# Gated DeltaNet layer on one core: the output weights' second half is prepared behind stream tiles q and v0 instead of between them

## The reference, cut to what matters

```
mod = silu(c) @ ada_w + ada_b;  shift, scale, gate = split(mod)
h = rms_norm(x) * (1 + scale) + shift
q, k, v, z, b, a = split(h @ w_in)         # 8 heads; q, k 128 wide, v, z 256 wide
q, k, v = silu(causal_conv4(q | k | v));   q, k = l2_norm(q) / sqrt(128), l2_norm(k)
per head, chunks of the sequence: invert (I + tril(beta k k^T * decay)), then
   S = state;  u = T (beta v - ... k S);  o = q S + (q k^T * decay) u;  S = S * g + k^T u
o = rms_norm(o) * silu(z)
out = rms_norm(x + gate * (o @ w_out))
```

## Time and profile before

| | |
|---|---|
| median of 3 runs | 1201.17 us (1200.78 to 1202.61) |
| the profiled execution | 1203.63 us, its span 1201.8 us |
| TensorE busy | 1114.4 us, 93% of the span |
| VectorE, GpSimd, ScalarE busy | 836.7, 599.9, 448.1 us |
| TensorE's granted clock, mean | 0.972 of full |

### The profile page before, as it was taken

How to read it: one execution, slowest core, us unless ns; L and a number is a source line. 1 busy time by engine, 2 the same in 40 slices (tenths; PEclk the granted TensorE clock), 3 DMA queues, 4 the chain that set the end, 5 groups by cost and what they waited for, 6 DMA issues and landing times.

```text
span 1201.8 us, 19507 instructions
## 1 busy us (share of the span) xinstructions
PE 1114.4 (93%) x5628; PEld 920.6 (77%) x5628; DVE 836.7 (70%) x1888; ACT 448.1 (37%) x1038; POOL 599.9 (50%) x819
## 2 busy tenths in 40 slices
PE   3896899999999999999999999999999999999984
PEld 2665688887888788887888788887888788887863
DVE  4776586776858586775858586685868677685835
ACT  4642333333242433433333333334243333334333
POOL 2353544565444744466345754456444853456413
PEclk9897899999999999999999999999999999999988
DMA  9922222213122321223221221223221222213103
GB/s 311 326 58 60 63 58 62 55 57 81 40 62 57 80 57 44 56 60 76 55 62 40 81 65 43 62 55 81 57 59 43 79 56 55 62 40 97 33 25 123
DMA packets 150754, 88.31 MB, mean 73 GB/s; under 512 B 29446, under 2 KB 145320, under 8 KB 150696
## 3 DMA queue, kind: packets, MB, share of 16 engines
q1 hardware_dynamic: 150696, 87.73, 26.6%
HBM read 78.28 MB, written 9.44 MB: 73 GB/s over the span
## 4 chain that ended last, share of the span: by engine, by line
PE 64%; POOL 12%; DVE 11%; issue 7%; ACT 2%; DMA 1%; SPq 0%; DVEq 0%; POOLq 0%; ACTq 0%
PE bank L406 31%; PE bank L506 11%; POOL w_lo L1344 5%; POOL wo_lo L1351 4%; DVE y L963 3%; DVE work L930 3%; PE bank L550 2%; PE bank L466 2%; PE bank L560 2%; PE bank L538 2%; PE bank L542 2%; PE bank L482 2%; PE bank L475 2%; PE bank L563 2%; PE bank L588 1%
## 5 line engine op out<-in xcount | busy, mean ns | idle before, releaser
L1344 POOL TENSOR_TENSOR w_lo<-w_raw,w_hi 128x256 fp32r<-128x256 f32 x384 | 333.5, 898 | 254.9 <-ACT w_hi L685 254.8
L406 PE MATMUL bank<-h_hi,w_hi 128*128 128x512 f32 x760 | 320.2, 421 | 20.8 <-POOL w_lo L1344 20.8
L406 PE MATMUL bank<-h_lo,w_hi 128*128 128x512 f32 x760 | 313.4, 412 | 0.0
L406 PE MATMUL bank<-h_hi,w_lo 128*128 128x512 f32 x760 | 310.6, 409 | 0.0
L406 PEld LDWEIGHTS bank<-h_hi,w_hi 128*128 128x128 f32 x760 | 146.5, 193 | 53.7 <-POOL w_lo L1344 24.8
L930 DVE SCALAR_TENSOR_TENSOR work<-pre,cw,work 128x512 f32<-128x512 f32 x192 | 168.5, 878 | 14.1 <-DVE work L927 5.4
L406 PEld LDWEIGHTS bank<-h_hi,w_lo 128*128 128x128 f32 x760 | 145.6, 192 | 30.8 <-issue 0.2
L406 PEld LDWEIGHTS bank<-h_lo,w_hi 128*128 128x128 f32 x760 | 146.9, 193 | 27.8 <-issue 0.2
L1394 POOL TENSOR_TENSOR og_lo<-work,og_hi 128x256 fp32r<-128x256 f32 x64 | 47.1, 737 | 217.4 <-ACT og_hi L745 217.4
L711 ACT ACTIVATE work<-work 128x512 f32<-128x512 f32 x64 | 40.2, 628 | 271.8 <-DVE pre L940 131.0
L506 PE MATMUL bank<-wo_hi,og_hi 128*128 128x512 f32 x256 | 113.7, 444 | 10.1 <-DVE y L963 10.1
(11 more groups left out here) (176 smaller groups left out, 1870.0 us busy)
## 6 DMA issues: line engine op xcount, KB each, us to landing
w_raw<-in_gdn_w_in SPq DMA_DIRECT2D x96, 512.0 KB, 4.0
work<-in_ada_w SPq DMA_DIRECT2D x8, 1024.0 KB, 9.7
w_raw<-in_gdn_w_out SPq DMA_DIRECT2D x16, 512.0 KB, 3.3
y<-in_x SPq DMA_DIRECT2D x8, 512.0 KB, 9.1
work<-in_ada_w SPq DMA_DIRECT2D x8, 512.0 KB, 6.1
n_dram<-work SPq DMA_DIRECT2D x16, 256.0 KB, 3.4
out<-y SPq DMA_DIRECT2D x8, 512.0 KB, 2.7
t_dram<-work SPq DMA_DIRECT2D x16, 64.0 KB, 1.6
```

Source lines behind the costliest of these rows:

```text
L406: mm = nc.tensor.matmul(bank[m % 2][:, :], w[:, m % 2, k, :], h[:, k, half, :], start=(r == 0), stop=(r == MM - 1))
L1344: i = nc.gpsimd.tensor_tensor(w_lo[:, k % 2, j:j + 2, :], w_raw_k[:, k % 2, j:j + 2, :], w_hi[:, k % 2, j:j + 2, :].bitcast(F32), ALU.subt ...
```

## The change

In even units wo1 moves. SyncE loads q and v0 right behind wo0, and wo1 behind `invert_out` and the `split_lo` of q, into slot 0 as before; v1 keeps slot 1, and the next unit's tile 0 is loaded only when wo1's low part is done. q and v0 swap slots, so `split_hi` and `split_lo` take the slot from the table. GpSimd gates wo1 in chunk 0 behind `split_lo` 4 and makes its low part in chunk 1 behind `og_low` 0 and ahead of `split_lo` 5. ScalarE rounds wo1 in chunk 1 behind `og_high` 0 and ahead of `split_hi` 5. Odd units and TensorE's and VectorE's programs stay.

```diff
-        RAW_EVEN = {0: (0, 1), 1: (1, 1), 2: (0, 2), "wo0": (1, 2), "wo1": (0, 3), 3: (1, 3), 4: (0, 4), 5: (1, 4)}
+        RAW_EVEN = {0: (0, 1), 1: (1, 1), 2: (0, 2), "wo0": (1, 2), 3: (0, 3), 4: (1, 3), "wo1": (0, 4), 5: (1, 4)}
+        def raw_slot(hd, par, key):
+            return key % 2 if hd is None else (RAW_ODD if par else RAW_EVEN)[key][0]
@@ SyncE, body
                     load_wo(hd, 0)
                     passed(sp, "w_lo_done", u, 3)
-                    load_wo(hd, 1)
+                    load_tile(0, q_cols(nxt))
                     wo_passed(sp, "wo_lo_done", hd, 1)
-                    load_tile(1, q_cols(nxt))
-                    wo_passed(sp, "wo_lo_done", hd, 2)
-                    load_tile(0, v_cols(nxt, 0))
+                    load_tile(1, v_cols(nxt, 0))
...
                 invert_out(u + 1)
                 passed(sp, "w_lo_done", u, 4)
-                load_tile(1, v_cols(nxt, 1))
-                passed(sp, "w_lo_done", u, 5)
+                if par == 0:
+                    load_wo(hd, 1)
+                    passed(sp, "w_lo_done", u, 5)
+                    load_tile(1, v_cols(nxt, 1))
+                    wo_passed(sp, "wo_lo_done", hd, 2)
+                else:
+                    load_tile(1, v_cols(nxt, 1))
+                    passed(sp, "w_lo_done", u, 5)
                 load_tile(0, z_cols(nxt, 0) if final else k_cols(hd + 1) if par else (hd * DK) + (HEADS + 1) * DK)
@@ ScalarE, body
                     decay_exp(u + 1)
-                    if par == 0:
-                        split_wo(hd, 1, u)
                     evacuate_z(u, 1, 0)
                     split_hi(u, hd, par, 3)
...
                         elif c == 1:
+                            if par == 0:
+                                split_wo(hd, 1, u)
                             split_hi(u, hd, par, 5)
@@ GpSimd, body
                         split_wo(hd, 0)
-                        gate_wo(hd, 1)
                     norm_k(u + 1)
                     mask_decay(u + 1)
-                    if par == 0:
-                        split_wo(hd, 1)
-                    split_lo(u, 3)
+                    split_lo(u, 3, raw_slot(hd, par, 3))
                 for c in range(NCH):
                     if not last and c == 0:
-                        split_lo(u, 4)
+                        split_lo(u, 4, raw_slot(hd, par, 4))
+                        if par == 0:
+                            gate_wo(hd, 1)
                     if c > 0:
                         og_low(u, c - 1)
                     if not last and c == 1:
+                        if par == 0:
+                            split_wo(hd, 1)
                         split_lo(u, 5)
```

More of the change, by code:

```diff
@@ L684, in split_hi @@
                 passed(act, "projected", u, k - 1)
-                nc.scalar.activation(w_hi[:, k % 2, :, :], w_raw_k[:, k % 2, :, :], ACT.Copy
+                nc.scalar.activation(w_hi[:, k % 2, :, :], w_raw_k[:, raw_slot(hd, par, k), :, :], ACT.Copy
                                      ).then_inc(S["w_hi_done"], 1)
@@ L1338, in row_power, with split_lo @@
                                         ).then_inc(scale_done, 1)
-            def split_lo(u, k):
+            def split_lo(u, k, raw=None):
                 passed(pool, "w_hi_done", u, k + 1)
                 passed(pool, "projected", u, k - 1)
+                raw = k % 2 if raw is None else raw
                 for j in range(0, KT, 2):
-                    i = nc.gpsimd.tensor_tensor(w_lo[:, k % 2, j:j + 2, :], w_raw_k[:, k % 2, j:j + 2, :],
+                    i = nc.gpsimd.tensor_tensor(w_lo[:, k % 2, j:j + 2, :], w_raw_k[:, raw, j:j + 2, :],
                                                 w_hi[:, k % 2, j:j + 2, :].bitcast(F32), ALU.subtract)
```

## The result

The changed kernel takes 1208.58 us, median of 4 runs (1207.42 to 1210.72), beside 1200.97 for the kernel before: a ratio of 1.006 with a 95% interval of 1.0046 to 1.0073. It is slower by some 7.6 us; 1202.0 had been forecast, with a range up to 1204.8. The profiled execution took 1207.42 us, 3.8 more than the one of before.

What follows compares the result with a forecast made beforehand. TensorE, busy 93%, was taken to bound the kernel. Per head 2.67 - 2.47 = +0.20 (unit 0 about +0.3) gave +1.7 us, less 0.9 for the clock: +0.8, so median 1201.17 to 1202.0, range 1197.8 to 1204.8.

Steps and rivals of the forecast that it cites:

- the old wait: Chunk 0 of even units: TensorE's wait for tile 3 (q), a 2.47 us delay plus 1.7 of clock, vanishes 8 times.
- the new wait at `out_project`: Head of chunk 2, even units: TensorE waits for wo1's low part, delay 2.67 us, idle 2.32, replacing the 2.47.
- No wait for tile 5 or for the next unit's tile 0: Behind the new low part: tile 5 keeps 2.0 us of slack, the next unit's tile 0 2.9; priced at 0.
- the gate: Gate of wo1 on GpSimd behind tile 4: ends about 491.5 to 492, hidden by GpSimd's own idle time, no cost.
- the clock: Behind each new gap TensorE drops to half speed, costing 1.7 us; half a head's worth allowed off, -0.9.
- The first rival: New gap at out_project passes without the clock drop in most heads: 1197.8 (three heads) to 1189.3 (all eight); chance 0.20.
- The second: Rival: wo1's low part in chunk 1 costs 4.26 us beside convolution taps, delay 3.67, time 1210.9; chance 0.13.

Runs made afterwards that it cites:

- e3: Changed kernel with wo1 rounded on ScalarE ahead of og_high 0 and its low part on GpSimd ahead of og_low 0: 1193.07 us.
- e1: Changed kernel with GpSimd's gate of wo1 made to wait until VectorE has made r of chunk 1: 1201.04 us.
- e2: Changed kernel with the gate of wo1 left out but for one instruction on 4 columns: 1200.3 us.
- e5: e1 with TensorE's decay_exponents matmul done three times instead of once in even units: 1213.24 us.
- e4: Kernel before with only wo1's rounding and low part moved, directly behind q's and ahead of tile 4, gate in its old place: 1182.05 us.

## Why the prediction was wrong

- **Right: where the old wait goes.** Tile 3 is asked for 0.68 us behind the state products and is ready.
- **Right: the new wait at `out_project`.** Idle time of 2.32 us was forecast, 2.29 measured, 8 times; low part 3.26 forecast for its place, 3.22 measured; e3 shows that the chain behind `og_high` makes it. No wait for tile 5 or for the next unit's tile 0 came up, as forecast: L413's waits for `w_lo` are down to 3.4 us, ahead of unit 0.
- **Wrong: the gate.** The step reads "Hidden by GpSimd's own idle time". That was true of GpSimd and said nothing of what GpSimd's work does to VectorE beside it. The prediction used the sharing one way only, for what VectorE does to the low part's duration, and passed over the trace's own signs of the other way: the same block-inversion lines have durations from 0.16 to 0.72 us in the kernel before, one of 0.72 at the very place. So `r`, which TensorE's next product needs, was taken to stand at its old distance. Priced at 0, the gate costs 1.83 us per head, 8 x 1.83 = 14.6 us. With that one thing taken away (e1, e2) the kernel comes to 1201.0 and 1200.3, beside the 1202.0 forecast. That closeness is partly chance: e1's gaps are longer than the 2.3 forecast, and both profiles have fewer drops than assumed.
- **Wrong, and helping: the clock.** A drop behind 7 to 8 of the 8 gaps was assumed. Without the wait at L557 it was 6 of 8 in either profile (e1, e2), and 4 of 8 where the units were longer (e5); with it 2 and 3 of 8. Some five drops fewer than forecast give back 5 x 1.7 = 8.5 us of the 14.6. No term of the prediction joins the drops to the gate, so this was luck: with the drops that it assumed the miss would have been 15 us and not 6.6.
- **The sum again,** per head against before: +0.1 to +0.2 for the longer gap (waits of 18.3 us in all against some 17.4), +1.8 for L557: 8 x 2.0 = 16. Five to six drops fewer than the 8 of before are 8.5 to 10. That leaves +6 to +7.5 where the medians show +7.6 and the two profiled executions +3.8. In those two the loop fits, +4.4 us behind unit 0 where 7 x 2.0 - 6 x 1.7 is 3.8; what differs lies ahead of it, since the changed one ends unit 0 at 177.08 and the other at 177.38, although its two waits there ought to put it some 2 us behind. Why stays open. The counts of drops are from one execution of the kernel before and two of the changed one, and the mean clock of the former's other executions goes from 0.972 to 0.986, so the part of the clock in this sum is an estimate. The gate's part is shown by e1 and e2.
- The first rival, gaps without the drop, came true in its mechanism and not in its time, since the unforeseen wait more than ate it. The second, a low part of 4.26, did not happen.

## What to carry to other kernels

When a step is moved to an engine's idle time, read what the engine beside it does in that stretch, and price the neighbour's slowdown too: GpSimd's idle time was free, VectorE's short steps were not, and r stood behind them. A step that feeds a wait must end ahead of it by its whole chain: moving only wo1's rounding and low part, and those a short way (e4), gained 20 us where moving all of its steps lost 7.6. That e4 is the better order is measured; how much of its gain is the gate's place and how much the low part's was not separated. And a saving in TensorE's wait is worth counting with its clock, which can take it back (e1) or give it (e3).

## What the runs showed that was not expected

- VectorE's tensor_tensor on 32 partitions with 48 to 60 columns takes 0.65 to 0.72 us beside GpSimd's tensor_tensor of 128x256 (0.7 to 0.8 us each) and 0.20 to 0.21 otherwise: about one GpSimd instruction's length each, at each of these sizes. It is not any work of GpSimd: beside `power_o`'s instructions on one column (415.64 to 416.44 in e1) the steps shown there take 0.20 to 0.21. The Trainium skill (GPSIMD Engine Reference, section Key points) names contention of the two engines with VectorE instructions that have two SBUF inputs, as these have; the trace agrees and gives its size, a factor of 3 on short ones.
- Gaps of equal length need not have equal drops of the clock: of 8 gaps of 2.29 us 2 and 3 (the changed kernel), 6 (e2); of 8 of about 2.65 us, 6 (e1) and 4, every second one (e5). Behind the gaps of 1.62 at L557 there was none. Each count is of one profiled execution. What decides among the long ones stays open.
